# Expert panels in four pieces of 4 KB rows, and three and two buffers for the experts' results

## The reference, cut to what matters

```
h = h + concat([gmlp_mixer(...), hgrn2_mixer(...)]) @ w_out
n2 = rms_norm(h, norm2_gain)
# hier_moe: top-1 group, top-2 experts in it
out[e] = (silu(x_e @ w_gate[e]) * (x_e @ w_up[e])) @ w_down[e]   # w_gate, w_up: 1024x512, w_down: 512x1024
h = h + sum over the token's two experts of weight * out
h = rms_norm(h, final_gain)
# second block: conv mixer, dilated attention, final norm
```

## Time and profile before

| | us |
|---|---|
| median of 3 runs | 1691.72 (1691.12 to 1696.5) |
| the profiled execution's own time | 1686.87 |
| its span (first to last instruction) | 1685.1 |
| PE busy | 1413.6 (84%) |
| DVE busy | 691.9 (41%) |
| ACT busy | 480.6 (29%) |
| panels' and other loads on q1 | 295.77 MB, 44.1% of 16 engines' span |
| mean granted TensorE clock | 0.931 of full speed |

### The profile page before, as it was taken

The page is one execution under the profiler, slowest core; times in us unless marked ns, Lnnn a source line. Parts: engine busy times, 40 slices in busy tenths (PEclk is TensorE's granted clock), DMA queues, the critical chain, the costliest instruction groups (busy, mean ns, idle before and its releaser), DMA issues. The chain is left out here.

```text
span 1685.1 us, 24127 instructions
## 1 busy us (share of the span) xinstructions
PE 1413.6 (84%) x9624; PEld 1062.5 (63%) x9624; DVE 691.9 (41%) x1278; ACT 480.6 (29%) x753; POOL 42.0 (2%) x79
## 2 busy tenths in 40 slices
PE   6999998748757678876762999997999999999976
PEld 5786776525434344443432788876788888888865
DVE  4566756010101102101005565555436665656645
ACT  5552440001000001000005322233434454444432
POOL 2000000000000000000002110000000000000000
PEclk9998997979979889997885999997999999999988
DMA  8947335979969973597957355220221212121101
GB/s 345 392 140 260 130 144 201 384 285 387 399 259 426 418 307 124 217 427 291 417 225 280 139 200 200 113 100 27 100 100 51 96 55 88 62 100 51 51 0 63
DMA packets 38376, 339.27 MB, mean 201 GB/s; under 512 B 3784, under 2 KB 9800, under 8 KB 19400
## 3 DMA queue, kind: packets, MB, share of 16 engines
q1 hardware_dynamic: 24192, 295.77, 44.1%
q0 software_dynamic: 7200, 34.08, 5.7%
q10 hardware_dynamic: 6824, 7.15, 1.2%
HBM read 312.62 MB, written 24.38 MB: 200 GB/s over the span
## 5 line engine op out<-in xcount | busy, mean ns | idle before, releaser
L285 PE MATMUL ps<-ring,ar 128*32 128x256 f32 (+1 forms) x2048 | 208.5, 416 | 53.5 <-PEq L652 20.6
L285 PE MATMUL ps<-ar 128*32 128x256 f32 (+6 forms) x1454 | 211.6, 394 | 13.0 <-DVE ar L1638 6.8
L285 PE MATMUL ps<-b_NH,b_WH 128*128 128x512 f32 x704 | 187.0, 401 | 8.2 <-DVE b_NL L1347 4.5
L285 PEld LDWEIGHTS ps<-ring,ar 128*32 128x32 f32 (+1 forms) x2048 | 107.1, 118 | 134.2 <-issue 65.4
L1713 DVE TENSOR_TENSOR ar<-ar,ps 128x128 f32<-128x128 f32 x46 | 13.0, 287 | 420.5 <-ACT ar L1020 417.3
L285 PE MATMUL ps<-b_NH,b_WL 128*128 128x512 f32 x704 | 181.3, 393 | 0.0
L1280 DVE TENSOR_TENSOR b_WL<-ring,b_WH 128x1024 fp32r<-128x1024 f32 x112 | 136.6, 1221 | 99.4 <-ACT b_WH L834 99.3
L285 PE MATMUL ps<-b_NL,b_WH 128*128 128x512 f32 x704 | 173.7, 389 | 0.0
L834 ACT ACTIVATE b_WH<-ring 128x1024 fp32r<-128x1024 f32 x112 | 118.1, 1055 | 162.7 <-PE ps L285 158.3
L285 PEld LDWEIGHTS ps<-b_NH,b_WH 128*128 128x128 f32 x704 | 130.7, 191 | 36.9 <-ACT b_NH L891 9.0
L285 PEld LDWEIGHTS ps<-b_NH,b_WL 128*128 128x128 f32 x704 | 133.9, 190 | 28.1
(11 more groups left out here) (273 smaller groups left out, 1782.3 us busy)
## 6 DMA issues: line engine op xcount, KB each, us to landing
ring<-in_wts_dram SPq DMA_DIRECT2D x79, 2048.0 KB, 9.2
spare<-in_wts_dram SPq DMA_DIRECT2D x31, 2048.0 KB, 13.2
ar<-in_wts_dram SPq DMA_DIRECT2D x22, 2048.0 KB, 15.5
y_scratch<-gate POOLq DMA_DIRECT2D x15, 1024.0 KB, 26.3
ring<-in_wmod_dram SPq DMA_DIRECT2D x24, 512.0 KB, 4.9
ar<-in_wmod_dram POOLq DMA_DIRECT2D x24, 512.0 KB, 4.2
y_scratch<-ar ACTq DMA_DIRECT2D x50, 128.0 KB, 10.0
hres<-in_x_dram SPq DMA_DIRECT2D x4, 512.0 KB, 6.7
```

The source lines that it names most:

```text
L285: return pe.matmul(o, l, m, start=start, stop=stop, skip_group_check=True)
```

## The change

It has three parts. (1) The panels of the experts lie in DRAM as four pieces of 128 rows of 4 KB, one piece after the other, and a load takes from each piece one row per partition: 512 packets of 4 KB in place of 128 of 16 KB, the same bytes into the same places. Panels of the other stages stay as they were. (2) Results of main blocks go round three buffers (`y0`, `y1`, `y2`) that lie in the tensor gate, those of second blocks round two (`oy0`, `oy1`); ACT waits for the store of three experts ago, or two. Since DVE uses the same part of gate once before the experts, the first copy waits for `ovx`. (3) Semaphores `vgain` and `slot` go: the first shares `ws`, the second's signal comes before `ovx`, which was waited for already.

```diff
         sg = [area(9472 + 128 * j, 128) for j in range(3)]
...
-        ysb = [area(10624 + 256 * j, 256) for j in range(3)]
+        ysb = [gate[:, 1, 256 * j:256 * j + 256] for j in range(3)]
+        ysb2 = [area(10624 + 256 * j, 256) for j in range(2)]
...
-            act.dma_start(vg, row(R_VG, 512)).then_inc(S["vgain"], 16)
+            act.dma_start(vg, row(R_VG, 512)).then_inc(S["ws"], 16)
...
                 act.wait_ge(S["m_d2"], n + 1)
-                if n >= 2:
-                    act.wait_ge(S[f"y{s}"], 16 * (n // 2))
-                copy_y(s, 5).then_inc(S["m_y"], 1)
+                if n >= 3:
+                    act.wait_ge(S[f"y{n % 3}"], 16 * (n // 3))
+                elif n == 0:
+                    act.wait_ge(S["ovx"], 1)
+                copy_y(ysb[n % 3], 5).then_inc(S["m_y"], 1)
                 act.wait_ge(S["m_y"], n + 1)
-                store(n, s).then_inc(S[f"y{s}"], 16)
+                store(n, ysb[n % 3]).then_inc(S[f"y{n % 3}"], 16)
...
-                    if n:
-                        act.wait_ge(S["oy"], 16 * n)
-                    copy_y(2, 7).then_inc(S["o_y"], 1)
+                    if n >= 2:
+                        act.wait_ge(S[f"oy{n % 2}"], 16 * (n // 2))
+                    copy_y(ysb2[n % 2], 7).then_inc(S["o_y"], 1)
                     act.wait_ge(S["o_y"], n + 1)
-                    store(NE + n, 2).then_inc(S["oy"], 16)
+                    store(NE + n, ysb2[n % 2]).then_inc(S[f"oy{n % 2}"], 16)
                 with act.Else():
                     if n:
                         act.wait_ge(S["o_ht"], n)
                         act.wait_ge(S["o_y"], n)
-                        act.wait_ge(S["oy"], 16 * n)
+                    if n >= 2:
+                        act.wait_ge(S[f"oy{n % 2}"], 16 * (n // 2))
...
-                sp.dma_start(slots[place[i]], A["wts"][i, :, :]).then_inc(s_slot[place[i]], 16)
+                if i < P_MOE or i >= P_C0:
+                    sp.dma_start(slots[place[i]], A["wts"][i, :, :]).then_inc(s_slot[place[i]], 16)
+                else:
+                    sp.dma_start(slots[place[i]].rearrange("p (a c) -> p a c", a=4),
+                                 A["wts"][i, :, :].rearrange("(a q) (r c) -> (q r) a c", a=4, r=4)).then_inc(
+                                     s_slot[place[i]], 16)
...
+    for i in range(P_MOE, P_C0):
+        wp[i] = wp[i].reshape(128, 4, 1024).transpose(1, 0, 2).reshape(128, 4096)
```

More of the change, by code:

```diff
@@ L27 @@
 SEMS = """
-const gm yzero cols ws wsm vgain bias rt_w fgain rope
+const gm yzero cols ws wsm bias rt_w fgain rope
 hi lo wdone tok turn nh nl tta ttd
@@ L32 @@
 cs md hres mp mpd
-rt_pe rt_act lt mb ctl ovx wts12 slot gexp pc rx
+rt_pe rt_act lt mb ctl ovx wts12 gexp pc rx
 wm0 wm1 wm2 wm3 wn0 wn1
-m_e m_oh m_gx m_xt m_up m_sg m_hh m_d1 m_ht m_d2 m_y y0 y1
-o_up o_sg o_hh o_d1 o_ht o_d2 o_y oy
+m_e m_oh m_gx m_xt m_up m_sg m_hh m_d1 m_ht m_d2 m_y y0 y1 y2
+o_up o_sg o_hh o_d1 o_ht o_d2 o_y oy0 oy1
 t_e t_oh t_gx t_xg t_tx t_xt t_up t_sg t_hh t_d1 t_ht t_d2 t_y ty
@@ L1023, in copy_h, with copy_y, store @@
                 return act.activation(hT[s].rearrange("p a b -> p (a b)"), ps[:, b, 0:128], ACT.Copy)
[L1025 to L1030, removed]
+            def copy_y(y, b):
+                return act.activation(y, ps[:, b, 0:256], ACT.Copy)
+            def store(n, y):
+                return act.dma_start(y_d[n * CAP:(n + 1) * CAP, :].rearrange("t (q c) -> q t c", q=4), y)
             def store_third(u):
@@ L1095, in scalar_program @@
                         act.wait_ge(S["o_y"], n)
-                        act.wait_ge(S["oy"], 16 * n)
+                    if n >= 2:
+                        act.wait_ge(S[f"oy{n % 2}"], 16 * (n // 2))
                     act.sem_inc(S["o_ht"], 1)
                     act.sem_inc(S["o_y"], 1)
-                    act.sem_inc(S["oy"], 16)
+                    act.sem_inc(S[f"oy{n % 2}"], 16)
                 with act.If(third(n)):
@@ L1506, in vector_program @@
             head_inverse("hv", rv)
-            dve.wait_ge(S["vgain"], 16)
+            dve.wait_ge(S["ws"], 32)
             head_scale("hv", VV, rv, vg.rearrange("p (o c) -> p o c", o=1).to_broadcast([128, 4, 512]))
@@ L1720, in vector_program @@
             pick_in(128, OH, "m_oh")
-            signals(dve.tensor_copy(slot_i, sl_f), "slot")
+            signals(dve.tensor_copy(slot_i, sl_f))
             signals(dve.tensor_tensor(oc, bc(mid(incl), 128, NOV, 32), bc(last(ji[:, 0:NOV]), 128, NOV, 32), ALU.is_le))
@@ L2031, in gpsimd_program @@
                 pool.memset(v[0:64, :, 64:128], 0.0).then_inc(S["scm_po"], 1)
-            pool.wait_ge(S["ws"], 16)
+            pool.wait_ge(S["ws"], 32)
             pool.memset(wsT[64:128, :, 0:64], 0.0).then_inc(S["wsm"], 1)
@@ L2075, in gpsimd_program @@
                     pool.wait_ge(S["ty"], 32 * (NE + j + 1))
-            pool.wait_ge(S["slot"], 1)
             pool.wait_ge(S["ovx"], 1)
@@ L2079, in gpsimd_program @@
             pool.wait_ge(S["m_y"], NE)
-            pool.wait_ge(S["y0"], 16 * (NE // 2))
-            pool.wait_ge(S["y1"], 16 * (NE // 2))
-            pool.wait_ge(S["oy"], 16 * NE)
+            for j in range(3):
+                pool.wait_ge(S[f"y{j}"], 16 * len(range(j, NE, 3)))
+            for j in range(2):
+                pool.wait_ge(S[f"oy{j}"], 16 * (NE // 2))
             pool.wait_ge(S["ty"], 32 * NE)
@@ L2156, in expert @@
                     def expert(s, k, e0_=e0_):
-                        return sp.dma_start(ov[s].rearrange("p (o c) -> p o c", o=1), A["wts"][
-                            bass.ds(e0_ + k, 1), :, :].rearrange("o p c -> p o c"))
+                        return sp.dma_start(ov[s].rearrange("p (a c) -> p a c", a=4), A["wts"][
+                            bass.ds(e0_ + k, 1), :, :].rearrange("o (a q) (r c) -> (q r) (o a) c", a=4, r=4))
                     if j == 0:
@@ L2175, in sync_program @@
             sp.wait_ge(S["m_hh"], NE)
-            sp.wait_ge(S["y0"], 16 * (NE // 2))
-            sp.wait_ge(S["y1"], 16 * (NE // 2))
-            sp.wait_ge(S["oy"], 16 * NE)
+            for j in range(3):
+                sp.wait_ge(S[f"y{j}"], 16 * len(range(j, NE, 3)))
+            for j in range(2):
+                sp.wait_ge(S[f"oy{j}"], 16 * (NE // 2))
             sp.wait_ge(S["ty"], 32 * NE)
```

## The result

| | before | changed |
| --- | --- | --- |
| median of the runs | 1691.42 us (4 runs, 1687.07 to 1696.5) | 1634.47 us (4 runs, 1630.98 to 1636.44) |
| profiled execution, and its span | 1686.9, span 1685.1 | 1636.44, span 1634.7 |
| ratio, 95% interval | | 0.966, 0.963 to 0.969 |

The forecast was 1645 in 1608 to 1690. The gain came where it was forecast. Between the profiled executions it was 3.4 us larger (50.4 for 47), between the medians 10 us: the sum added 4.9 us for the median, and this time the median lay 2 us under the profiled execution. Three single executions in the experiments took far longer (1926 to 3631 us, one of them of the kernel before), and the ratios leave them out.

What follows compares the result with a forecast made beforehand. Slow 128 KB stores were taken to hold ACT, then PE and loads. The experts' three pieces summed to a stage end at 839, 47 us earlier: 1686.9 to 1640, plus 4.9 for the median: 1645 us, range 1608 to 1690.

Steps and rivals of the forecast that it cites:

- lower bound of one to one: Experts' stores: at least one 4 KB load packet (0.16 us) passes per store packet, at most four.
- Rival B: Experts' stores: turns go by bytes, stores still take 19.5 us with loads queued; about 1668 us, chance 0.11.
- Rival C: Experts' loads: 4 KB reads half a megabyte apart fall below 409 GB/s; gain gone from 5.75 us a panel; chance 0.12.
- Rival D: Experts' stage: stalls return everywhere as waits for panels, nothing is left; within 5 us of 1692, chance 0.05.
- add nothing, and cost nothing: Third and second result buffers: no gain once stores land before ACT asks, and no cost.
- first piece: Experts 0 to 17: 47 panels at 5.1 us, 36 us for stores, 7 us besides; ends at 577, 36 us earlier.
- The second: Experts 18 to 20, two with third blocks: no change, 92 us.
- The third: From expert 23's first load at 669: 27 panels at 5.1 us, 21 for stores, 3, 3 and 5; ends at 839.
- In 3 to 8 us: Experts' stores with 4 KB load packets: landing time, 1.7 to 5.5 us for 8 packets plus 2 us of start.
- a panel in 5.1 to 5.5 us in full stretches: Sign of the forecast in the experts' loads: a panel lands every 5.1 to 5.5 us where loads are full.
- instruction fetches included: Experts' stage: each store takes 1.5 us of DMA engine time from the loads, instruction fetches counted in.
- SP has time: Issue of loads on SP: stays at one instruction a load, and SP has time for it.

Runs made afterwards that it cites:

- e1: Changed kernel with its 4 KB rows but the old two buffers for main blocks and one for second blocks: 1635.03 us, 0.970 of the time before.
- e5: Changed kernel with a partition's four 4 KB pieces 4.25 KB apart in one DRAM row, not 512 KB apart: 1631.57 us, 0.967 of the time before.
- e2: Changed kernel with its new buffers, but the experts' panels loaded in 16 KB rows as before: 1658.63 us, 0.983 of the time before.
- e8: Changed kernel with 8 KB rows and the old two buffers for main blocks, one for second blocks: 1652.48 us, 0.979 of the time before.
- e7: Changed kernel with each main block's store issued twice, the second time to a spare tensor: 1672.33 us, 0.993 of the time before.
- e3: Changed kernel with two pieces of 8 KB rows instead of four of 4 KB, new buffers kept: 1624.79 us, 0.963 of the time before.
- e6: Changed kernel with eight pieces of 2 KB rows instead of four of 4 KB: 1657.82 us, 0.983 of the time before.
- e10: Changed kernel with 8 KB rows and main blocks' stores issued by SP in the loads' own queue: 1623.57 us, 0.964 of the time before.

## Why the prediction was right, point by point

**What held.** The four views named the right wait, its cause, and what was late next. Stores' turns go by packets. At 16, 8, 4 and 2 KB of load packets, one store packet takes 2.4, 1.33, 0.82 and 0.52 us. That is four load packets (0.61, 0.31, 0.16 and 0.08 us) and 0 to 0.2 us more; what is added matters at the small sizes, and so the count is 4.3, 4.4, 4.5 and then 6.2 to one. The lower bound of one to one that the prediction took from the earlier trace rows was borne out nowhere. Rival B, the turn by bytes, is refuted by that row of numbers and by the waits of e1. Rival C, reads half a megabyte apart, is refuted by e5 and by the packets of 159 ns. Rival D, nothing left, by the result. The buffers' "add nothing, and cost nothing" is shown at 4 KB by e1, and by e2 and e8 not to hold at 16 and 8 KB.

**Two pieces to a microsecond, one 7 us too long.** In the first piece, 46 panels from landing to landing took 304.3 to 576.4, 272.1 us, where the terms 46 x 5.1 + 36 gave 271. The second was 92 us for 92. The third was given 170 and took 163. From the issue at 669.2 the first panel took 9.6 us, the 26 others 150.7, and the last product 2.4. The panels' 27 x 5.1 are 138 of that in both; the rest was put at 32 (21 for stores, 3, 3 and 5) and was 25. The mis-sized term is what stood beside the loads: the 14 stores from 683.7 us on took 18 us (150.7 less 26 x 5.1) and not 21, and the 3, 3 and 5 were 7.

**A store lands later than was said.** "In 3 to 8 us" was 10.6. The first packet moves 3.9 us after the issue where loads are queued, where I had put 2 us, and the turn took 6.7, above the 5.5 of four packets alone (medians of the stores issued from 300 to 560 us). The trace of before had that 3.9 too, so it could have been read there. It changed nothing, since ACT asks an expert later at the earliest, 17 us. At 8 KB 3.9 us and two stores of 10.6 behind one another are past that, and e8 missed: its expectation had stores up to an expert late, but put only 1 to 15 us on it.

**A mark that contradicted its own sum.** The prediction wanted a panel in 5.1 to 5.5 us in full stretches. The mean was 5.9, and its own terms, 47 x 5.1 + 36 over 47, already said so. Most panels with no store beside them do land 5.0 to 5.3 apart, and from 680 to 690 us q1 moved 4.03 MB at 99.7%, 404 GB/s for the 409 named.

**4% for 4 KB.** The loads alone took 4.9 us a panel at 16 KB, 5.0 at 8, 5.1 at 4 and 5.3 at 2 KB. The fixed 3 cycles of the Trainium skill (DMA: Bandwidth & Descriptors, "Why small descriptors are slow (HBM only)") would give an estimated 1.7% from 16 to 4 KB; the traces show the 4% that the sum used.

**What remains open** is why 128 packets of 1 KB cost the loads 1.2 to 1.5 us. I split 320 to 560 us of the change's trace into microseconds by what else moved, and took the mean rate of q1. "A store" is a microsecond in which one of its 1 KB packets began, "a fetch" one in which, or in the two before it, an instruction fetch (q8) began:

| beside the loads | us | q1, GB/s |
| --- | --- | --- |
| neither | 60 | 399 |
| a fetch | 32 | 375 |
| a store | 78 | 370 |
| both | 70 | 332 |

Of the 45 us below 330 GB/s, 28 have both, 10 a store alone, 4 a fetch alone and 3 neither. A store of 6.7 us costs about 0.6 us by that table, half of the 1.2 that e7 shows for one more. The rest of the prediction's 1.5 "instruction fetches included" is where its words put it, but no run took the fetches away, so this is a reading and not shown.

## What to carry to other kernels

Where small stores share the DMA engines with a deep queue of loads, as here, a store's time was its packets per engine times four load packets and up to 0.2 us each: choose the load's row so that a store lands before its buffer is wanted. Smaller than that only costs the loads; with more buffers a larger row can win, up to a point (8 KB with three and two: 1624 us, 4 KB: 1635, 16 KB: 1659, 2 KB: 1658). Two edits that take away the same wait don't add, so each should be tried alone, and a buffer that is worth nothing at one packet size can be worth 28 us at another. Before adding buffers, look at how long the issues last: at 16 KB a store's issue held ACT for up to 14 us once more stores stood in the queue.

## What the runs showed that I had not expected

The SP engine no longer issues a load in a third of a microsecond. The timeline of its loads in the change, from 440 us on (start, length, runs of equal ones together), and its line there as a group (shortest/median/longest ns):

```profile
441.22 10.53 SPq L2121 DMA_DIRECT2D ar<-in_wts_dram  x1
451.83 11.50 SPq L2121 DMA_DIRECT2D ring<-in_wts_dram  x2
463.44 5.85 SPq L2121 DMA_DIRECT2D ar<-in_wts_dram  x1
469.38 15.70 SPq L2121 DMA_DIRECT2D spare<-in_wts_dram  x3
```

```profile
L2121 SPq DMA_DIRECT2D ring<-in_wts_dram x4: 911/5570/6476, 433.4 to 458.4; - x4
```

With four to five panels under way a load's issue lasts as long as a panel takes to land: each of the 48 issues over 1.9 us in the stage's loads ends when three earlier panels are left to land. At 8 KB (e3) five are left at the end of such an issue, at 2 KB (e6) two in 70 cases of 78, and at 16 KB, with up to four panels under way, no issue takes that long. The page's median time to landing rises to 25 us for the spare and arena buffers. It costs nothing here, since the DMA engines are full in that time, but what stands behind such a load on SP would come 5 to 10 us late, and in e2 the same thing on ACT, with stores, stood in the way of silu. My prediction's "SP has time" was true for another reason than it gave.

A store costs the loads about its price in e10 as well, where its packets stand in the loads' own queue. And the price isn't one for the bytes: 0.34 us for 64 packets of 2 KB against 1.2 for 128 of 1 KB. What sets it stays open; it falls by more than the number of packets does.
